# A hybrid encoder layer on one Trainium2 core: who issues the stores of the gated activations, and when

## The reference, cut to what matters

```python
x = x + (0.5 * swiglu(rmsnorm(x, norm_ffn1), w1_gate, w1_up, w1_down))
y, new_state = token_mix(rmsnorm(x, norm_mix), p, past)
x = x + y
x = x + (0.5 * swiglu(rmsnorm(x, norm_ffn2), w2_gate, w2_up, w2_down))

def swiglu(h, w_gate, w_up, w_down):
    return (silu(h @ w_gate) * (h @ w_up)) @ w_down
```

## Time and profile before

| | |
|---|---|
| median of 3 runs | 2081.39 us (2081.07 to 2082.53) |
| the profiled execution | 2079.68 us |
| its span, first to last instruction | 2077.9 us |
| TensorE busy | 2002.1 us, 96% |
| VectorE busy | 1201.8 us, 58% |
| ScalarE busy | 775.1 us, 37% |
| GpSimd busy | 247.1 us, 12% |
| moved by DMA | 265.01 MB, mean 128 GB/s |
| up projection of the first mixing | about 34 to 497 us |
| its down projection | about 497 to 703 us |
| up projection of the second mixing | about 1360 to 1832 us |
| its down projection | about 1832 us to the end |

### The profile page before, as it was taken

One profiled execution on the slowest core, in us unless ns is written; L12 is line 12 of the kernel. 1 busy time (PEld: TensorE's weight loads), 2 busy tenths in 40 slices (PEclk: granted clock), 3 DMA queues, 4 the chain that ended last, 5 costly groups with the idle time before them and its releaser, 6 DMA issues.

```text
span 2077.9 us, 35766 instructions
## 1 busy us (share of the span) xinstructions
PE 2002.1 (96%) x15115; PEld 1937.1 (93%) x15115; DVE 1201.8 (58%) x1649; ACT 775.1 (37%) x1252; POOL 247.1 (12%) x302
## 2 busy tenths in 40 slices
PE   6999999999999989889999999989999999999999
PEld 5999999999999979668789979989999999989999
DVE  6856555656676662455554284277555565576674
ACT  5433333334333342554142293244333333333231
POOL 0000000000000340251121062200000000000000
PEclk9999999999999999999999999999999999999999
DMA  4222322226965422211011124212222222387664
GB/s 151 83 99 84 126 84 97 87 106 250 384 223 194 167 115 98 96 33 42 22 43 41 47 67 157 106 68 79 112 98 85 99 108 103 114 325 294 239 213 163
DMA packets 66287, 265.01 MB, mean 128 GB/s; under 512 B 7564, under 2 KB 20220, under 8 KB 56656
## 3 DMA queue, kind: packets, MB, share of 16 engines
q1 hardware_dynamic: 51248, 198.89, 26.4%
q0 software_dynamic: 14880, 63.83, 7.9%
HBM read 203.52 MB, written 59.18 MB: 126 GB/s over the span
## 4 chain that ended last, share of the span: by engine, by line
PE 78%; issue 11%; DVE 4%; ACT 3%; DMA 3%; POOL 1%; SPq 0%; DVEq 0%; POOLq 0%; ACTq 0%
PE ps L169 72%; PE ps L1258 1%; DVE sb_nrm L292 1%; POOL sb_rms L189 1%; DMA sb_h_raw<-h_kept 1%; DMA sb_down_raw<-wb 1%; ACT sb_pr L1360 1%; DVE sb_h_lo L927 1%; DMA sb_h_first_raw<-h_kept 1%; PE ps L1835 0%; PE ps L1829 0%; PE ps L1588 0%; PE ps L1847 0%; PE ps L1566 0%; DMA sb_x<-x 0%
## 5 line engine op out<-in xcount | busy, mean ns | idle before, releaser
L169 PE MATMUL ps<-sb_xh,sb_up_hi 128*128 128x272 f32 x2432 | 702.8, 289 | 10.9 <-DVE sb_xl L399 10.9
L169 PE MATMUL ps<-sb_xl,sb_up_hi 128*128 128x272 f32 x2432 | 703.0, 289 | 0.0
L169 PE MATMUL ps<-sb_xh,sb_up_lo 128*128 128x272 f32 x2432 | 701.0, 288 | 0.0
L169 PEld LDWEIGHTS ps<-sb_xh,sb_up_hi 128*128 128x128 f32 x2432 | 460.7, 189 | 12.8 <-DVE sb_xl L399 12.8
L169 PEld LDWEIGHTS ps<-sb_xh,sb_up_lo 128*128 128x128 f32 x2432 | 460.1, 189 | 0.0
L169 PEld LDWEIGHTS ps<-sb_xl,sb_up_hi 128*128 128x128 f32 x2432 | 459.9, 189 | 0.0
L169 PE MATMUL ps<-sb_h_hi,sb_down_hi 128*128 128x272 f32 x1188 | 343.2, 289 | 4.2 <-DVE sb_down_lo L872 3.9
L169 PE MATMUL ps<-sb_h_hi,sb_down_lo 128*128 128x272 f32 x1188 | 344.0, 290 | 0.0
L169 PE MATMUL ps<-sb_h_lo,sb_down_hi 128*128 128x272 f32 x1188 | 342.1, 288 | 0.0
L169 PE MATMUL ps<-sb_nh,sb_whi 128*128 128x362 f32 (+1 forms) x696 | 231.0, 332 | 7.1 <-ACT sb_fq L1109 4.4
L169 PE MATMUL ps<-sb_nl,sb_whi 128*128 128x362 f32 (+1 forms) x696 | 229.6, 330 | 0.0
(11 more groups left out here) (311 smaller groups left out, 2685.1 us busy)
## 6 DMA issues: line engine op xcount, KB each, us to landing
sb_down_raw<-wb SPq DMA_DIRECT2D x92, 704.0 KB, 5.2
sb_up_raw<-wa SPq DMA_DIRECT2D x44, 1024.0 KB, 4.8
sb_h_raw<-h_kept SPq DMA_DIRECT2D x60, 544.0 KB, 5.9
sb_wraw<-wm SPq DMA_DIRECT2D x17, 1024.0 KB, 4.8
h_kept<-sb_hs_b POOLq DMA_DIRECT2D x20, 816.0 KB, 4.7
h_kept<-sb_hbuf POOLq DMA_DIRECT2D x42, 272.0 KB, 2.3
h_kept<-sb_hs_a POOLq DMA_DIRECT2D x20, 544.0 KB, 3.2
sb_h_first_raw<-h_kept SPq DMA_DIRECT2D x10, 544.0 KB, 4.4
```

Of the source, the lines that this page charges most:

```text
L169: mm = K.nc.tensor.matmul(out, a, b, start=first and n == 0, stop=last and n == 2, skip_group_check=loose)
```

## The change

`up_pool` no longer stores anything; it keeps the waits and the reload of `x`. A function `h_store` with the same four transfers for pair j is called by ACT: in `up_act` after product P5 of each even tile c, behind that product's copy and cast, with j = c/2 - 1, so for pairs 0 to 9; and in `down_act` in group 0, between `down_hi` of group 1 and the casts of chunks 6 and 7, for pair 10. The first transfer no longer has a wait of its own: both activation stores wait for all four halves of the pair. Both channel mixings do this. Sources, destinations, sizes and semaphores are the same.

```diff
+        if q == P5 and c % 2 == 0:
+            h_store(K, e, N, hs, c // 2 - 1)
         if c == FT - 1:
...
-def up_pool(K, e, N, hs, x_src):
-
-    def store(j):
-        e.wait_ge(N.f.h, N.was.h + 4 * j + 1)
-        e.dma_start(hs[0, :, j], h_block(K, j, 0, 0)).then_inc(N.f.hst[0], 16)
-        e.wait_ge(N.f.h, N.was.h + 4 * j + 4)
-        e.dma_start(hs[1, :, j], h_block(K, j, 1, 1)).then_inc(N.f.hst[1], 16)
...
-    for j in range(KF - 1):
-        store(j)
-    store(KF - 1)
+def h_store(K, e, N, hs, j):
+
+    e.wait_ge(N.f.h, N.was.h + 4 * j + 4)
+    e.dma_start(hs[0, :, j], h_block(K, j, 0, 0)).then_inc(N.f.hst[0], 16)
+    e.dma_start(hs[1, :, j], h_block(K, j, 1, 1)).then_inc(N.f.hst[1], 16)
+    e.wait_ge(N.f.hsum, N.was.hsum + 5 * j + 5)
+    a, b = (K.hs_a_last, K.hs_b_last) if j == KF - 1 else (K.hs_a, K.hs_b)
+    e.dma_start(hs[2:4, :, j].rearrange("i p t -> p i t"), a[:]).then_inc(N.f.hss, 16)
+    e.dma_start(hs[4:7, :, j].rearrange("i p t -> p i t"), b[:]).then_inc(N.f.hss, 16)
+
+
+def up_pool(K, e, N, x_src):
     e.wait_ge(N.f.hclo, N.was.hclo + NCH)
...
         if g + 1 < GROUPS:
             down_hi(K, e, N, g + 1)
+        if g == 0:
+            h_store(K, e, N, hs, KF - 1)
         if p + 1 < NP:
```

More of the change, by code:

```diff
@@ L578, in up_start_act, with up_act @@
     xsum_hi(K, e, N, X_T3, 1)
-def up_act(K, e, N):
+def up_act(K, e, N, hs):
     nc = K.nc
@@ L954, in down_pe, with down_act @@
         mm.then_inc(N.f.grp, 1)
-def down_act(K, e, N, follow=None):
+def down_act(K, e, N, hs, follow=None):
     for g in range(GROUPS):
@@ L2602, in _ @@
             first_act(K, e, F1)
-            up_act(K, e, F1)
+            up_act(K, e, F1, o["h_kept"])
             nc.scalar.preload_act_table_set(LOG_EXP)
-            down_act(K, e, F1, follow_down)
+            down_act(K, e, F1, o["h_kept"], follow_down)
             norm_act(K, e, M.norm)
@@ L2620, in _ @@
             up_start_act(K, e, F2)
-            up_act(K, e, F2)
-            down_act(K, e, F2)
+            up_act(K, e, F2, o["h_kept"])
+            down_act(K, e, F2, o["h_kept"])
         @block.vector
@@ L2675, in _ @@
         def _(e):
-            up_pool(K, e, F1, o["h_kept"], x_in)
+            up_pool(K, e, F1, x_in)
             down_pool(K, e, F1, x_in)
@@ L2711, in _ @@
             follow_pool(K, e, F2)
-            up_pool(K, e, F2, o["h_kept"], o["x_kept"])
+            up_pool(K, e, F2, o["x_kept"])
             down_pool(K, e, F2, o["x_kept"])
```

## The result

The changed kernel takes 2087.49 us in the median of 19 runs, the kernel before 2081.64 in 19 runs beside them: ratio 1.0028, 95% interval 1.0021 to 1.0036. It is 5.9 us slower, more than the 0.2% that a measurement can tell from no change. Its profiled execution took 2090.71 us, with a span of 2088.9. That is 3.2 us above its median; the profiled execution of the kernel before lay 2.0 us under the median of its 19.

A forecast was written before the change was run, and what follows sets the result against it. TensorE, 96% busy, was taken to bound the kernel. Terms 0 + 1.2 + 0.7 = 1.9 us gave 2081.6 from the profiled execution, 2083.3 from the median, put at 2083.4; range 2079.4 to 2087.6 us.

The forecast's parts named there:

- Part one: Up projections: ACT issues twenty of twenty-two store sets, 1.6 us each, all covered; price 0, up to 21 x 1 us.
- Issue cost and the casts: First mixing's passage to the down projection: ACT's issues start the cast of chunk 6 1.15 us later, at 510.5.
- rival (B): Passages: ACT held up by its issues, 1.0 us or more each; 7.1 us together, 2086.8 or 2088.5; chance 0.20.
- The 0.5 us term: First mixing's passage: DVE ends the remainders of chunks 6 and 7 0.5 us later, reaching TensorE through chunk 9.
- The bytes: Passages: 272 KB of activation enter the full DMA stretch, 0.7 us for all loads behind; the other three stores cost nothing.
- the 0.7 us forecast there: Second mixing's passage: 0.7 us of bytes on a chain of transfers up to the last gap, nothing for ACT.
- The reload: First mixing: POOL's reload of x may land 1.2 us later unseen; beyond that it costs microsecond for microsecond.
- The clock: Low clock around a TensorE gap costs 1.7 us; if the gap at 529.85 grows to 2.9 us, 2085.1.
- the 0.74 for no measurable difference: Whole kernel: chance 0.74 that the time measures the same, within about 0.2%, 4.2 us.
- (C): Passages: the last store of sums lands up to 3.9 us sooner off POOL's path; faster, 2077.5 us; chance 0.06.

The follow-up runs named there:

- wide pieces: The changed kernel, but the last pair's five sums go to a scratch of their own, in pieces of 4352 and 6528 bytes: 2084.05 us, 1.0015.

## Why the prediction was right and wrong

**The square.** Moment and issuer of the last set, as ratios to the kernel before:

| | early activation stores | late, next to the sums |
|---|---|---|
| POOL issues | 1.0000 (before) | 1.0013 (1.0005 to 1.0022) |
| ACT issues | 1.0003 (0.9993 to 1.0012) | 1.0028 (1.0021 to 1.0036) |

Landing of the last store in the first mixing: 9.4 and 9.9 us in the left column, 11.6 and 13.5 in the right. The moment is what costs: 544 KB of activations put right in front of the sums, in a stretch where the DMA engines are full. Who issues matters only there, by about as much again, and the wide pieces take that part away (11.5 us, 1.0015). The split is approximate, as the intervals reach about 2 us to each side. That the smaller packets are the reason for ACT's part is supported by that one kernel alone; it also moved the place of the sums in HBM, and its loss stood at another gap. The landings of the second mixing speak for it too: 9.9 us from POOL late, 14.5 from ACT late, 10.7 in wide pieces. What makes POOL's packets larger is open.

A rival carrier is the load of chunk 11, which waits for the last store as the reload does. The trace of the changed kernel speaks against it: the load left at 523.81 in place of 520.23, but landed after 4.3 us in place of 11.3, and ACT cast that chunk at 533.80 in place of 533.84. And the kernel with only the reload late has the whole loss without any store later.

**Part one: right.** TensorE is at 453.00 of 453.00 us, ACT's issues in the up projection take 0.34 to 0.52 us behind tile 20's P5, the cast after them has 1.95 us of idleness in front as before, and twenty sets by ACT measure 1.0002. That set is one of the cheap ones: by the medians of the four issues (0.34, 0.46, 0.48 and 1.04 us) a set takes 2.3 us, where 1.6 was forecast, and the nine microseconds of the casts behind it cover the rest. The landing of an activation store grew from 2.3 to 6.0 us in the median (7.5 at most for an even tile's in the up projections), which the 7.8 us until `hbuf` is written again still cover; that margin was thinner than the 2.3 us from the rows of before made it look.

**Issue cost and the casts: the rows right, the price wrong.** The issues in the passage took 0.34, 0.45, 0.38 and 0.80 us, 1.97 together, under the 3 us from which rival (B) decides. The cast of chunk 6 started at 511.19 in place of 509.35, 1.8 us later (forecast 1.15). But the gap at 529.8 did not grow, 1.56 for 1.67 us (forecast 2.9), and ACT early, with the same late casts, costs nothing. The 0.5 us term was worth 0. DVE ended the remainders of the two chunks at 514.81 in place of 513.70, so 1.1 us late (forecast 0.5), and was back in step one chunk later, at 523.86 for 523.90, as it had 4.40 us of waiting there before and has 3.25 now.

**The bytes: the step that failed.** "Moved inside it they cost nothing while the engines stay full" looks at the sum of the traffic and not at the order in it, and POOL's kernel with only the two activation stores moved measures 1.0013. I priced 272 KB at 0.7 us, shared by everyone behind. What was delayed was one transfer: the landing of the last store, from 9.4 to 13.5 us and from about 520.2 to 523.8, so by 3.6 us, five times the term. In the second mixing it landed after 14.5 us in place of 7.9, and there POOL's reload, issued at 1870.62, still met its update without a gap behind it: the last gap is 2.19 us for 2.22. It stands 44.7 us behind the last gap of the first group in place of 42.9, with a new gap of 0.59 us at 1875.24 on the way, and the granted clock behind it is 1.00 over 10 us where it was 0.83. The two nearly cancel, and the stage took 0.4 us more, within what two executions differ by. So the 0.7 us forecast there is neither borne out nor refuted.

**The reload: the sentence that was one row short.** The prediction names the whole path: stores, reload, update. It then says that the reload may land 1.2 us later unseen, because TensorE would be that late too. The row for it was in the trace of before: the remainder behind the update ends at 538.06 and TensorE's group is due at 538.10. TensorE was not late (529.80 for 529.85), so the slack was 0.04 us in place of 1.2, and 5.7 us of delay (3.6 from the landing, 2.1 from the longer reload) gave a gap of 5.44. "Beyond that it costs microsecond for microsecond" is what happened.

**The clock: right in kind.** The low clock came behind the gap that had become long, 0.66 over 8 us, some 2.3 us by the count of matmuls, where the bound was 1.7. The gap for which the bound had been set kept 1.00 in the changed kernel at 1.56 us, and had 0.83 over 10 us behind it at 2.77 us with the wide pieces.

**The time.** 2087.49 lies in the range, 0.1 us under its upper end, and on the forecast's side. That is luck: the upper end came from rival (B), whose cause did not occur. The forecast of 2083.4 was 4.1 us short, and the 0.74 for no measurable difference rested on it. The time is nearly the one of rival (B), 2088.5, by another mechanism: ACT's issues in the passage took 1.97 us together, and the casts behind them came 1.8 us later at no cost. (C) is refuted, 13.5 us where under 6 would have been its mark; so the Trainium skill's starvation of GpSimd-issued transfers (SBUF — State Buffer, "SBUF: two separate sides") has nothing to explain here, and the measurement of POOL early and ACT early at 1.0000 and 1.0003 agrees with its other rule (DMA: Bandwidth & Descriptors, "Issuing engines are not separate DMA queues"), that another issuing engine saves no more than the time of issuing.

## What to carry to other kernels

When a store is moved, follow not the issuer's time but who waits for the landing, link by link up to the bounding engine, and read the slack of the last link from two rows: when the operand is ready and when the matmul wants it. Here it was 0.04 us in the execution read, behind a semaphore that makes one large reload wait for a store that it does not need. Taking that wait away is no cure by itself: in a full DMA stretch a large transfer sent 4 to 5 us earlier cost at least as much here as one sent 4 to 5 us later (1.0043 and 1.0031), so its place in the order is to be tuned, and measured.

## What the runs showed of the hardware that was not expected

- **Packets.** The same stores, with rows of 2176 bytes, went in packets of 3.8 KB in the mean when POOL issued them and of 2.03 KB when ACT did. Beside full traffic the last store took 11.6 and 9.9 us (first and second mixing) from POOL at the same moment, 13.5 and 14.5 from ACT, and 11.5 and 10.7 from ACT in wider pieces. The Trainium skill (DMA: Bandwidth & Descriptors, "Queues, rings and completion order") has each DMA engine turn from queue to queue packet by packet, by which smaller packets would get a smaller share, if its packets are those that are counted here. The landings agree with that, and with early stores no difference in time was seen.
- **Issues on ACT are uneven.** In the up projections the fourth issue of a burst has a median of 1.04 us and up to 1.73, the second 0.455 with one of 1.8. TensorE has no gap there. Durations in ns, min/median/max:

```profile
L755 ACTq DMA_DIRECT2D h_kept<-sb_hs_b x20: 492/1042/1732, 91.8 to 1814.3; - x20
L751 ACTq DMA_DIRECT2D h_kept<-sb_hbuf x22: 450/455/1815, 88.0 to 1852.4; - x22
```

- **On ACT an issue ran beside the computation ahead of it, and the one behind it waited.** ACT's first store was issued at 506.71, while the cast that stands ahead of it in program order ran from 506.70 to 508.07. The cast behind the four issues began at 511.19, just after the last of them (510.29 + 0.80): of the 3.11 us of idleness ahead of it 1.8 were the wait for DVE's sums and 1.2 the two issues.
- **The same transfer took quite different times by what stood beside it.** The 2.2 MB reload took 14.3 us to land in the kernel before and 16.4 in the changed one, 13.7 there without the lower half behind it, but still 14.9 without it in the kernel before; the chunk of 544 KB took 8.1 us with the reload sent 6.1 us after it, and 14.8 with the reload sent 2.1 us after it.
